# All convolution taps on VectorE, alternating between channel tiles, with the latent projections moved ahead of the last channel pair

## The reference, cut to what matters

```python
h = rms_norm(x, norm1_g[l]) * (1.0 + scale1) + shift1      # scale, shift, gate: c_act @ w_ada + b_ada
proj = jnp.einsum('bsd,dk->bsk', h, w_in[l])
c_q, c_kv = proj[..., :256], proj[..., 256:384]            # the latents
k_rope = proj[..., 384:448]
conv_u = proj[..., 448:]                                   # 2 x 512 channels
attn_out = mla_group(c_q, c_kv, k_rope, cos, sin, ...)     # 4 heads, 192 wide keys, softmax
# conv_group(conv_u):
y = a * jax.nn.sigmoid(g)                                  # a, g: the halves of conv_u
y = depthwise convolution of y over the tokens, 31 taps, + conv_b
conv_out = jax.nn.silu(layer_norm(y, conv_norm_g, conv_norm_b))
mix = concatenate([attn_out, conv_out]) @ w_out[l]
x = x + gate1 * mix                                        # then the expert block
```

## Time and profile before

| what | value |
|---|---|
| median of 3 runs | 2745.37 us (2745.16 to 2750.52) |
| the profiled execution | 2745.22 us, of which the span of the trace is 2743.5 us |
| TensorE busy | 2494.7 us, 91% |
| VectorE busy | 1108.6 us, 40% |
| ScalarE busy | 923.7 us, 34% |
| GpSimd busy | 413.7 us, 15% |
| VectorE's taps (L1019) | 170 in both layers, 182.1 us, mean 1071 ns |
| layer 0: tile 1's first matmul, the rotation's first instruction on VectorE | 61.23 us, 201.42 us |
| layer 1: the same two | 891.85 us, 1034.35 us |

### The profile page before, as it was taken

One profiled execution on the slowest core, in us unless ns is written; L12 is line 12 of the kernel. 1 busy time (PEld: TensorE's weight loads), 2 busy tenths in 40 slices (PEclk: granted clock), 3 DMA queues, 4 the chain that ended last, 5 costly groups with the idle time before them and its releaser, 6 DMA issues. The chain is left out here.

```text
span 2743.5 us, 32074 instructions
## 1 busy us (share of the span) xinstructions
PE 2494.7 (91%) x12958; PEld 1491.6 (54%) x12958; DVE 1108.6 (40%) x1606; ACT 923.7 (34%) x1275; POOL 413.7 (15%) x192
## 2 busy tenths in 40 slices
PE   5869979999997869879999996999999999989998
PEld 4633623333334743633333333787788797766665
DVE  4976231221223877231121123566422102446665
ACT  3435311111113335321111113656523344335553
POOL 0522000000000432000000002000334362200000
PEclk8979889999998979989999997999999999989999
DMA  9600569999999520378999997222123341139995
GB/s 332 233 28 1 195 267 371 410 410 409 410 409 332 198 76 0 147 285 342 410 410 410 410 409 236 77 77 92 63 97 101 100 146 46 62 119 373 361 353 212
DMA packets 276276, 646.27 MB, mean 236 GB/s; under 512 B 12097, under 2 KB 110655, under 8 KB 276159
## 3 DMA queue, kind: packets, MB, share of 16 engines
q1 hardware_dynamic: 269038, 631.78, 61.4%
q0 software_dynamic: 2592, 7.87, 0.8%
q10 hardware_dynamic: 4528, 4.98, 0.5%
HBM read 639.88 MB, written 6.29 MB: 236 GB/s over the span
## 5 line engine op out<-in xcount | busy, mean ns | idle before, releaser
L740 PE MATMUL ps<-ring,scr 128*64 128x512 f32 x1952 | 425.8, 593 | 3.3 <-DMA ring<-in_w_up 1.9
L740 PEld LDWEIGHTS ps<-ring,scr 128*64 128x64 f32 x1952 | 138.5, 137 | 279.3 <-issue 272.9
L1410 POOL TENSOR_TENSOR raw_r<-raw,w_high 128x2048 fp32r<-128x2048 f32 (+1 forms) x44 | 192.4, 4379 | 465.9 <-ACT w_high L1664 465.9
L762 PE MATMUL ps<-ring,scr 128*64 128x512 f32 x1024 | 231.9, 606 | 1.4 <-ACT scr L955 1.4
L461 POOL TENSOR_TENSOR one_hot_T_r<-hy,one_hot_T_r 128x1024 fp32r<-128x1024 f32 x16 | 38.5, 2407 | 1134.5 <-ACT one_hot_T_r L969 1134.5
L1426 PE MATMUL ps<-x_high,w_high 128*128 128x512 f32 x480 | 194.6, 405 | 10.4 <-DVE xT_r L1881 5.3
L1428 PE MATMUL ps<-x_high,raw_r 128*128 128x512 f32 x480 | 191.1, 398 | 0.0
L1427 PE MATMUL ps<-xT_r,w_high 128*128 128x512 f32 x480 | 190.7, 397 | 0.0
L1019 DVE SCALAR_TENSOR_TENSOR one_hot_T<-h_tok,convw,one_hot_T 128x512 f32<-128x512 f32 x170 | 182.1, 1071 | 9.0
L1186 DVE SCALAR_TENSOR_TENSOR xT<-ps,mod,xT 128x512 f32<-128x512 f32 x128 | 86.5, 744 | 219.1 <-PE ps L728 218.4
L2536 DVE TENSOR_TENSOR ring_r<-ring,ring_high 128x2048 fp32r<-128x2048 f32 x56 | 127.6, 2289 | 58.3 <-ACT ring_high L2414 58.2
(11 more groups left out here) (519 smaller groups left out, 4681.8 us busy)
## 6 DMA issues: line engine op xcount, KB each, us to landing
ring<-in_w_down SPq DMA_DIRECT2D x64, 2048.0 KB, 16.4
ring<-in_w_up SPq DMA_DIRECT2D x62, 2048.0 KB, 19.6
ring<-in_w_gate SPq DMA_DIRECT2D x60, 2048.0 KB, 16.3
ring<-in_w_up SPq DMA_DIRECT2D x56, 1024.0 KB, 7.3
ring<-in_w_ada SPq DMA_DIRECT2D x22, 2048.0 KB, 12.9
ring<-in_w_down SPq DMA_DIRECT2D x28, 1024.0 KB, 7.1
raw<-in_w_in SPq DMA_DIRECT2D x23, 1024.0 KB, 5.1
ring<-in_w_in SPq DMA_DIRECT2D x16, 512.0 KB, 10.9
```

Source lines behind the costliest of these rows:

```text
L740: mm = pe.matmul(ps[CAP * half:CAP * (half + 1), 1 + j // 2, :], x_e[:, at_x:at_x + CAP], weights[:, k, half * HALF:(half + 1) * HALF], st ...
L762: mm = pe.matmul(ps[CAP * half:CAP * (half + 1), 4, :], hidT[:, at_f:at_f + CAP], weights[:, k, half * HALF:(half + 1) * HALF], start=(j = ...
L1410: pool.tensor_tensor(dst, src, high.bitcast(F32), ALU.subtract).then_inc(w_ready, 1)
```

## The change

All 124 taps of a layer go to VectorE; ScalarE's products and GpSimd's additions go. The first 14 taps are of channel tile 0 alone, then two tiles alternate, so that a tap waits (`conv_tap`) for the one before the last instead of the last. 79 taps follow the work of the projection tiles, 24 the last of it, and 21 stand in the attention's steps 0 to 5. The projection's order becomes 0 to 5, 8 to 11, 6, 7 (`IN_ORDER`). The latents' sums come after the tenth tile, their inverse and spread between the eleventh and twelfth, and their scaling before VectorE's last projection work. The mean of the convolution moves to the attention's step 7 and another bank, the rest of its layer norm moves behind it. The one load of the latents' weights (1792 KB) moves up in the DMA queue, from behind chunk 7 to between the chunks 5 and 6.

```diff
-POOL_TAPS = {1: TAPS, 3: 6}
-TAPS_A_TILE = 5
-DVE_TAPS = (0, 11, 11, 9, 0, 10, 11, 10, 0)
+IN_ORDER = (0, 1, 2, 3, 4, 5, 8, 9, 10, 11, 6, 7)
+ALONE = 14
+TAPS_IN_TILE = (0, 5, 9, 9, 10, 10, 10, 10, 6, 4, 2, 4)
+TAPS_IN_HEADS = 24
+TAPS_IN_STEP = (4, 4, 4, 3, 3, 3)
...
+def tap_order():
+    left, out = [list(range(TAPS)) for _ in range(CT)], []
+    for _ in range(ALONE):
+        out.append((0, left[0].pop(0)))
+    for c in range(CT - 1):
+        while left[c]:
+            out += [(c, left[c].pop(0)), (c + 1, left[c + 1].pop(0))]
+    return out + [(CT - 1, t) for t in left[CT - 1]]
...
-            for piece, then in ((2, (5, 6)), (3, (7,)), (CT, range(8, 12))):
+            for piece, then in ((2, (5,)), (CT, (6,)), (3, range(7, 12))):
...                                                     # GpSimd
-            for c, taps in POOL_TAPS.items():
-                for t in range(1, taps):
-                    pool.wait_ge(prod_ready, n + 1)
...
-                    pool.tensor_tensor(acc[:, c, :], acc[:, c, :], products[n % 3], ALU.add).then_inc(prod_used, 1)
...                                                     # TensorE, behind the matmuls of a tile
+                if at_tile == 9:
+                    pe.wait_ge(ada_rows, 12)
+                    for k in range(3):
+                        pe.wait_ge(lat_sq, k + 1)
+                        grouped_sum(6, P * (k // 2), scr[:, k, :], k != 1, k != 0).then_inc(lat_ss, 1)
+                if at_tile == 10:
+                    pe.wait_ge(mod_ready, 3)
+                    pe.wait_ge(lat_inv, 1)
+                    broadcast(7, root2[:, 0:P]).then_inc(lat_bc, 1)
+                    broadcast(6, root2[:, P:2 * P]).then_inc(lat_bc, 1)
             pe.wait_ge(uq_in, 48)
             pe.wait_ge(lat_ready, 3)
             for i in range(14):
+                if i < 5:
+                    pe.wait_ge(act_proj, 4 + i)
                 if i == 5:
-                    pe.wait_ge(act_proj, 8)
+                    pe.wait_ge(dve_proj, CT)
...                                                     # TensorE, attention
-            for c in range(CT):
-                mm = pe.matmul(ps[:, 5, :], ones[:], acc[:, c, :], start=(c == 0), stop=(c == CT - 1))
-            mm.then_inc(cmean, 1)
...
+                if i == 7:
+                    pe.wait_ge(conv_tap, CT * TAPS)
+                    for c in range(CT):
+                        mm = pe.matmul(ps[:, 7, :], ones[:], acc[:, c, :], start=(c == 0), stop=(c == CT - 1))
+                    mm.then_inc(cmean, 1)
+                if i == 11:
                     pe.wait_ge(csq, CT)
...
-                if i == 8:
+                if i == 13:
                     pe.wait_ge(cinv, 1)
...                                                     # ScalarE
+                if at_tile == 9:
+                    for n, width in enumerate((Q_RANK, KV_RANK)):
+                        act.wait_ge(lat_ss, 3)
+                        act.activation(root2[:, n * P:(n + 1) * P], ps[:, 6, n * P:(n + 1) * P], ACT.Sqrt, ...
...
-                if 1 <= i <= CT:
-                    act.wait_ge(cdev, i)
-                    act.activation(scr[:, i - 1, :], acc[:, i - 1, :], ACT.Square).then_inc(csq, 1)
-                if i == 6:
+                if i in (8, 9):
+                    for c in (2 * (i - 8), 2 * (i - 8) + 1):
+                        act.wait_ge(cdev, c + 1)
+                        act.activation(scr[:, c, :], acc[:, c, :], ACT.Square).then_inc(csq, 1)
+                if i == 11:
                     act.wait_ge(cvar, 1)
...                                                     # VectorE
+                for n, (c, t) in enumerate(tap_order()):
...
+                        dve.wait_ge(conv_tap, last[c])
+                        op = dve.scalar_tensor_tensor(acc[:, c, :], src, w, acc[:, c, :], ALU.mult, ALU.add)
+                    op.then_inc(conv_tap, 1)
+                    last[c] = n + 1
+                    yield
...
+            for at_tile, i in enumerate(IN_ORDER):
+                if at_tile == 4:
                     modulation(1).then_inc(mod_ready, 1)
+                if at_tile == 9:
+                    step(modulation(2))
...
+                if at_tile == 10:
+                    dve.wait_ge(lat_root, 2)
+                    dve.reciprocal(root2, root2).then_inc(lat_inv, 1)
+                if at_tile == 11:
+                    dve.wait_ge(act_proj, 6)
+                    dve.wait_ge(lat_bc, 2)
+                    for n in range(2):
+                        dve.scalar_tensor_tensor(cq[:, n, :], cq[:, n, :], ..., ps[:, 7, :], ...).then_inc(lat_ready, 1)
+                    dve.scalar_tensor_tensor(ckv, ckv, vec[:, KVG:KVG + 1], ps[:, 6, :], ...).then_inc(lat_ready, 1)
+                if i < 2 * CT and i % 2 == 1:
...
+                    dve.tensor_tensor(ypad[:, c, PAD:PAD + S], ps[:, at_tile % 6, :], sig, ALU.mult).then_inc(dve_proj, 1)
+                if at_tile + 3 < IN_TILES and at_tile != 6:
+                    w_in_rest(at_tile + 3)
+                for _ in range(TAPS_IN_TILE[at_tile]):
+                    next(conv)
+                if at_tile == 6:
+                    w_in_rest(9)
+            for _ in range(TAPS_IN_HEADS):
+                next(conv)
...                                                     # VectorE, attention
+                if i < len(TAPS_IN_STEP):
+                    for _ in range(TAPS_IN_STEP[i]):
+                        next(conv)
+                if i in (7, 8):
                     dve.wait_ge(cmean, 1)
...
-                if i == 7:
+                if i == 12:
                     dve.wait_ge(croot, 1)
...
-                if 9 <= i < 9 + CT:
+                if i in (14, 15):
                     dve.wait_ge(cbc, 1)
                     dve.wait_ge(csq, CT)
```

More of the change, by code:

```diff
@@ L285, in layer @@
     h_high = M["hy_r"][:, KT * S:2 * KT * S].rearrange("p (k n) -> p k n", k=KT)
-    products = [one_hot_T[:, 3 * KT * P + i * S:3 * KT * P + (i + 1) * S] for i in range(2)] + [scr[:, 3, :]]
     first = Q_RANK + KV_RANK + ROPE
@@ L850, in _ @@
             w_in_split_tile(2)
-            conv = conv_products()
-            for i in range(IN_TILES):
-                act.wait_ge(proj, i + 1)
-                bank = i % 6
-                if i < 2 * CT:
-                    if i % 2 == 0:
-                        if i >= 2:
-                            act.wait_ge(dve_proj, i // 2)
-                        act.activation(sig, ps[:, bank, :], ACT.Sigmoid).then_inc(act_proj, 1)
-                    ada_kept(4 + i, 6)
-                elif i < 11:
+            for at_tile, i in enumerate(IN_ORDER):
+                act.wait_ge(proj, at_tile + 1)
+                bank = at_tile % 6
+                if i < 2 * CT and i % 2 == 0:
+                    if i >= 2:
+                        act.wait_ge(dve_proj, i // 2)
+                    act.activation(sig, ps[:, bank, :], ACT.Sigmoid).then_inc(act_proj, 1)
+                if at_tile < 8:
+                    ada_kept(4 + at_tile, 6)
+                if 2 * CT <= i < 11:
                     n = i - 2 * CT
@@ L1043, in _ @@
             conv = convolve()
-            for i in range(IN_TILES - 3):
-                if i == 4:
+            for at_tile, i in enumerate(IN_ORDER):
+                if at_tile == 4:
                     modulation(1).then_inc(mod_ready, 1)
-                if i % 2 == 1 and i < 2 * CT:
-                    c = i // 2
-                    dve.wait_ge(act_proj, c + 1)
-                    dve.wait_ge(proj, i + 1)
-                    dve.tensor_tensor(ypad[:, c, PAD:PAD + S], ps[:, i % 6, :], sig, ALU.mult).then_inc(dve_proj, 1)
-                w_in_rest(i + 3)
-                for _ in range(DVE_TAPS[i]):
-                    next(conv, None)
@@ L1055, in _ @@
-            step(modulation(2))
-            step.settle()
-            dve.scalar_tensor_tensor(smod[:, KT:2 * KT], mod[:, SCALE2:SCALE2 + KT], 1.0, vec[:, N2G:N2G + KT], ALU.add, ALU.mult).then_inc(mod_ready, 1)
-            dve.wait_ge(lat_root, 2)
-            dve.reciprocal(root2, root2).then_inc(lat_inv, 1)
-            dve.wait_ge(act_proj, 7)
-            dve.wait_ge(lat_bc, 2)
-            for i in range(2):
-                dve.scalar_tensor_tensor(cq[:, i, :], cq[:, i, :], vec[:, QLG + i:QLG + i + 1], ps[:, 7, :], ALU.mult, ALU.mult).then_inc(lat_ready, 1)
```

138 lines of the change are left out of this document (48 added, 90 removed).

## The result

The changed kernel takes 2697.08 us (median of 4, 2694.99 to 2701.39) against 2747.64 us before on the same chip: ratio 0.9818, 95% interval 0.98 to 0.9835, so about 50 us less. Predicted were 2685 us, in a range of 2668 to 2713. The profiled execution has a span of 2694.7 us, 48.8 less than before.

A forecast was written before the change was run, and what follows sets the result against it. VectorE's taps, slowed to 2.1 times by GpSimd, were taken as the critical path from the second projection tile to the rotation. 39.0 + 41.3 - 2 x 9.9 = 60.5 us gave 2685 us, in a range of 2668 to 2713.

The forecast's parts named there:

- The projection and the heads: From tile 1 to the rotation: rotation at 162.4 and 993.0, gaining 39.0 us in layer 0 and 41.3 in layer 1.
- alternating taps 0.66 apart: VectorE's taps: one waiting for the one before the last costs 0.66 us, within bounds of 0.60 and 0.784.
- no wait for a weight rest or for modulation: TensorE in the projection: all waits on VectorE's weight rests go, and modulation(1), made at 93.8, precedes its use at 97.5.
- one wait for the inverse: Before the latents' spread, TensorE is ready at 132.5 and waits 2.9 us for the latents' inverse at 135.4.
- Alternation buys nothing: Rival: a tap stays at 0.784 us, costing 13.6 us a layer, 2712 us in all; chance 0.12.
- The attention gave back: Behind the rotation, the attention loses 7.6 + 0.8 + 1.5 = 9.9 us a layer, with 6 and 17.5 as ends.
- A start 1.8 us earlier: Attention's start: without the mean's matmuls in front, rotation to first row maximum takes 12.6 us instead of 14.4.
- meeting GpSimd: Attention's last nine taps: some meet GpSimd's `w_out` rests, costing 1.5 us a layer, within bounds of 0 and 9.1.
- the moved norm: Later attention: variance's matmuls (1.08 us) now stand behind the ninth scores; two scalings delay the last transposes by 0.8.
- its own terms: Low end of the range: taps at 0.60 us save 4.2 a layer (2677), no GpSimd meeting gives 2682, both 2671.
- Taking turns or an exclusive lock?: VectorE beside GpSimd: turns taken, 1.5 us a layer; a lock by whoever comes first would cost 7.6, 12 us in all.
- The clock rival: TensorE's clock falls in the attention's first six steps, costing 12 us a layer, 2709 us; chance 0.10.

The follow-up runs named there:

- The first experiment: The changed kernel with each tap waiting for the tap just before it, whichever channel tile that was of: 2722.67 us, ratio 0.9905.
- The filler experiment: The changed kernel with four unused 128x512 matmuls between the first key factor and the first scores: 2701.35 us, ratio 0.9814.
- The later splits: The changed kernel with ScalarE's splits of w_out, and so GpSimd's rests, in attention steps 6 to 13 instead of 3 to 10: 2698.29 us, ratio 0.9812.
- the filler's layer 1: The changed kernel with four unused products ahead of the first scores and two behind the scores of each of steps 0 to 5: 2696.95 us, ratio 0.981.
- 9 for GpSimd: The kernel before with all 124 taps of a layer on VectorE, each chained, without GpSimd's and ScalarE's share: 2740.08 us, ratio 0.9963.
- 22 for the spreading: The changed kernel with the attention's 21 taps ahead of the rotation instead, 45 there: 2719.13 us, ratio 0.99.
- three edits: Changed kernel with later w_out splits (2698.29 us); those with the rests on VectorE (2695.28); or taps over eight steps and a later norm (2695.18).
- two of them together: The changed kernel with the attention's taps in eight steps, a later norm, and w_out's rests on VectorE: 2684.4 us, ratio 0.9759.

## Why the prediction was right, and where not

**The projection and the heads: right.** Each step of that sum is in the trace: alternating taps 0.66 apart; no wait for a weight rest or for modulation, which is made at 91.87; one wait for the inverse, 2.43 where 2.9 were forecast; the heads' start to the rotation 161.76 - 142.41 = 19.4 us, as forecast (162.4 - 143.0). The gain to the rotation is 79.8 where 80.3 was predicted, and that it is so close is partly luck: layer 0 gained 1.1 us less than forecast and layer 1 0.6 more. In layer 0 tile 11 took 6.84 us instead of 5.5, since its first matmuls ran slow after the wait (0.63 instead of 0.39 us each); in layer 1, behind a wait of the same length, they didn't, and it took 5.55.

**"Alternation buys nothing": refuted.** The first experiment has the waits as the only difference and costs 24 to 26 us. The Trainium skill (VectorE: DVE Perf Modes, "The DRAIN you can't avoid") reports for eight copies in a row that a semaphore after each costs nothing extra; these taps pay 0.12 us each when the wait is for the operation just before. The same section also says that a next operation which is not held (not made to wait for all earlier ones) starts earlier, a sentence that the prediction passed over; the 0.66 us here agree with it.

**The attention gave back 33.7 and not 2 x 9.9.** This is the term that was mis-sized. The working had, in layer 0 / layer 1:
- A start 1.8 us earlier, which didn't come (1.6 / 1.9). The scores did start sooner behind the rotation (10.33 instead of 12.22 us), but took 3.79 us at half clock instead of 2.1. The mean's matmuls were costed as pure time on the path; that they also kept TensorE busy was not seen. The filler experiment shows the same trade: with them the clock holds, and the first maximum comes at the same time.
- 14 x 0.12 = 1.7 us: only 96 taps alternate. The last 14, of channel tile 3 alone, are 0.79 apart (the next instruction starts 3.14 us after the first of four, at 187.12) and were priced at 0.66. That was an oversight in reading `tap_order`, not a matter of the chip.
- 3.5 us for meeting GpSimd where 1.5 was taken (1.30 on the key diagonal, 2.15 on a tap). The later splits took exactly that away (7.74 to 4.3).
- 0.9 / 1.3 us in the steps behind the seventh maximum. This is the low clock in the seventh step, which costs 1.2 / 1.7 against the 4.35 us of the steps at full clock; behind the ninth maximum the filler's layer 1 takes 41.56 us as the changed kernel does (41.56 / 41.55), and the moved norm costs 0.4 less than was forecast.
- In layer 1 another 1.1 in the six steps, by the low clock in the second one.

That makes 6.2 / 8.0 us, for the 15.7 - 9.9 = 5.8 and 18.0 - 9.9 = 8.1 that were missing. The start and the last two terms are TensorE's clock, which the forecast had put at nothing.

One slip in the range: its own terms, 8.4 and 3.0 us less, give 2674 as the low end and not 2671.

**Taking turns or an exclusive lock?** The prediction took the 1.67 us spacing as taking turns and left the lock of the Trainium skill (SBUF — State Buffer, "SBUF: two separate sides") at the side. The rows speak for the lock: both slowed instructions ended 0.54 us after GpSimd's, however long it was, and the 1.67 seen before the change is the same 0.55 us behind an addition of 1.56. What they don't show is that the first to start gets it: the tap was recorded 0.01 us ahead of the rest and stood all the same. The working's reason for a small value, that GpSimd's operation fills at most half of a step, is void: what counts is whether an instruction falls behind it. But the 7.6 us that the rule was given was too much as well, since only two rests fell into the six steps, one of them when the diagonal was due and nearly half of it was over.

**The clock rival** (12 us a layer) had the mechanism and the wrong price. The clock did fall, twice. The rival assumed that every half-speed product lies on the path; with the clock held at 1.00 over the six steps, layer 0 was no faster, and with the clock held until some 10 us before the attention's end, layer 1 was 3.1 us faster.

What stays open: undoing the latents' order alone wasn't tried. Nor can it be had as a remainder: what was measured piece by piece (24 for alternating, 9 for GpSimd, 22 for the spreading) already adds up to more than the 51 us of the whole, so the pieces are not independent.

## What to carry to other kernels

Break a chain of dependent VectorE operations into two that alternate, and wait for the last but one. Before work is moved beside GpSimd, look which of its instructions can fall ahead of one with two SBUF inputs, and give their whole length to the price. When one of two contended spots is freed, look where the next one waits: here three edits gave nothing alone, and two of them together 12 us.

## What the runs showed of the hardware

- Scaled adds of 128x512 float32 that each wait for the one before are 0.787 us apart, and 0.66 when each waits only for the last but one; the duration is 0.75 either way. In the kernel before, the 25 taps behind the latents carry a second wait, and are 0.856 apart.
- A VectorE instruction with two SBUF tensor inputs stands until GpSimd's operation is over, then needs 0.54 to 0.55 us more at 128x512 (2.90 and 1.98 instead of 0.75 and 0.68; 1.67 before the change). A scaling of 0.49 us, with one SBUF input, took 1.36 to 2.14 in the changed kernel and ended 0.28 us after GpSimd. A maximum over PSUM and a product of one SBUF and one PSUM input weren't slowed (0.68).
- A wait of TensorE of 2.0 us was followed by scores of 2.07 instead of 1.12 us and a product of 4.90 instead of 3.70; a wait of 2.15 in another run by scores of 1.92 and 1.58 and an unslowed product of 3.60. A lowered clock lengthened a step by 1.2 to 1.7 us where TensorE was or became the bound, and by nothing in most steps that VectorE bounds.
